# Block-sparse attention in a hybrid decoder step: the sliding branch's weights scaled by GpSimd instead of VectorE

## What is computed

```python
p_c = masked_softmax(q @ k_cmp, block_end <= t)         # compressed keys
p_s = masked_softmax(q @ k_sel, s <= t)                 # "full" here
p_w = masked_softmax(q @ k_win, (s <= t) & (s > t - WINDOW))   # WINDOW = 512
o = g_c * (p_c @ v_cmp) + g_s * (p_s @ v_sel) + g_w * (p_w @ v_win)
```

## Time and profile before

| what | value |
|---|---|
| time, median of 3 runs | 2090.6 us (2086.77 to 2098.51) |
| the profiled execution, its own time | 2094.56 us |
| its span in the trace | 2092.8 us |
| `attend_prompt` in that span | about 407 to 767 us |
| TensorE busy over the span | 1826.2 us, 87% |
| VectorE busy over the span | 1113.8 us, 53% |
| GpSimd busy over the span | 119.7 us, 6% |

### The profile page before, as it was taken

How to read it: one execution, slowest core, us unless ns; L and a number is a source line. 1 busy time by engine, 2 the same in 40 slices (tenths; PEclk the granted TensorE clock), 3 DMA queues, 4 the chain that set the end, 5 groups by cost and what they waited for, 6 DMA issues and landing times. The chain is left out here.

```text
span 2092.8 us, 32262 instructions
## 1 busy us (share of the span) xinstructions
PE 1826.2 (87%) x12951; PEld 1691.3 (81%) x12951; DVE 1113.8 (53%) x1980; ACT 634.8 (30%) x1134; POOL 119.7 (6%) x143
## 2 busy tenths in 40 slices
PE   6999999677888868988794458999999999999998
PEld 6989999566677757777682248999999999999997
DVE  5462752367777754555345665844444554444454
ACT  6523311244554442333223323521112111121211
POOL 0000000000000021221202120000000000000000
PEclk9999999768999988999856679999999999999999
DMA  7621243400000025446252646311211111111102
GB/s 186 87 91 31 88 145 112 101 11 21 11 12 1 1 103 179 172 162 215 94 127 40 184 138 205 86 36 44 77 40 40 40 40 40 64 56 40 40 21 81
DMA packets 171473, 170.87 MB, mean 82 GB/s; under 512 B 49756, under 2 KB 156340, under 8 KB 167396
## 3 DMA queue, kind: packets, MB, share of 16 engines
q1 hardware_dynamic: 167892, 131.54, 22.3%
q0 software_dynamic: 2304, 33.56, 4.2%
q10 hardware_dynamic: 1168, 4.26, 0.9%
HBM read 136.98 MB, written 36.56 MB: 83 GB/s over the span
## 5 line engine op out<-in xcount | busy, mean ns | idle before, releaser
L58 PE MATMUL pm<-hidH,weights 128*128 128x344 f32 x768 | 247.7, 323 | 4.4 <-DVE weights L3151 4.4
L58 PE MATMUL pm<-hH,wuH 128*128 128x344 f32 x768 | 246.4, 321 | 3.4 <-DVE wuL L3146 3.1
L59 PE MATMUL pm<-hidL,weights 128*128 128x344 f32 x768 | 246.7, 321 | 0.0
L60 PE MATMUL pm<-hidH,weights 128*128 128x344 f32 x768 | 246.3, 321 | 0.0
L60 PE MATMUL pm<-hH,wuL 128*128 128x344 f32 x768 | 245.4, 319 | 0.0
L59 PE MATMUL pm<-hL,wuH 128*128 128x344 f32 x768 | 245.2, 319 | 0.0
L58 PE MATMUL pz<-hH,winH 128*128 128x344 f32 x600 | 201.2, 335 | 11.0 <-DVE zb L830 6.5
L60 PE MATMUL pz<-hH,winL 128*128 128x344 f32 x600 | 194.9, 325 | 0.0
L59 PE MATMUL pz<-hL,winH 128*128 128x344 f32 x600 | 194.8, 325 | 0.0
L3155 DVE SCALAR_TENSOR_TENSOR act<-pm,onat 128x344 f32<-128x344 f32 x96 | 49.3, 515 | 244.6 <-PE pm L60 244.5
L3166 DVE TENSOR_TENSOR onat<-pm,onat 128x344 f32<-128x344 f32 x256 | 129.0, 513 | 70.3 <-PE pm L60 70.3
(11 more groups left out here) (588 smaller groups left out, 3582.3 us busy)
## 6 DMA issues: line engine op xcount, KB each, us to landing
uact<-in_w_up_dram SPq DMA_DIRECT2D x16, 1024.0 KB, 6.8
hs<-in_w_down_dram SPq DMA_DIRECT2D x16, 1024.0 KB, 4.9
raw<-in_w_in_dram SPq DMA_DIRECT2D x24, 512.0 KB, 4.0
vS_scratch<-page_rows SPq DMA_DIRECT2D x16, 512.0 KB, 4.5
hold<-vS_scratch SPq DMA_DIRECT2D x8, 1024.0 KB, 12.3
wo<-in_w_out_dram SPq DMA_DIRECT2D x12, 512.0 KB
act<-in_w_out_dram SPq DMA_DIRECT2D x12, 512.0 KB, 4.1
onat<-qkT_scratch SPq DMA_DIRECT2D x18, 256.0 KB, 4.1
```

What stands on the lines that cost most here:

```text
L58: nc.tensor.matmul(out, wH, mH, start=(k == 0), stop=False)
L59: nc.tensor.matmul(out, wH, mL, start=False, stop=False)
L60: last = nc.tensor.matmul(out, wL, mH, start=False, stop=(k == n - 1))
```

## The change

In the VectorE list, the reciprocals now carry a semaphore of their own (`rs_ready`), and only the FULL columns are scaled there; `scaled` is raised by that instruction. GpSimd gets a loop over all units and heads: it waits for the reciprocals of the head and scales the WIN columns, raising `win_scaled`. TensorE waits, as before, for `scaled` at a unit's first group, and in addition for `win_scaled` of both heads at each group whose last tile is a WIN tile. The order of TensorE's and ScalarE's instructions is the same.

```diff
@@ gpsimd, behind the masks
+                for u, (i, kv, j) in enumerate(sched.units):
+                    for g in range(2):
+                        pool.wait_ge(rs_ready, 2 * u + g + 1)
+                        at, w = TILES(i, FULL) * P, TILES(i, WIN) * P
+                        gate = (kv * 4 + 2 * j + g) * 3 + WIN
+                        nc.gpsimd.tensor_scalar(pm[:, u % 2, g, at:at + w], pm[:, u % 2, g, at:at + w], rs[:, u % 2, g, 1:2],
+                                                gnat[:, i, gate:gate + 1], ALU.mult, ALU.mult).then_inc(win_scaled, 1)
@@ tensor, turn(n)
                     if kind != CMP and n == first + 1:
                         pe.wait_ge(scaled, sched.scaled_at[u + 1])
+                    if kind != CMP and pair[-1][0] == WIN:
+                        pe.wait_ge(win_scaled, 2 * u + 2)
@@ vector, scale_head(s)
-                    nc.vector.reciprocal(rs[:, u % 2, g, :], den[:, u % 2, g, :])
+                    nc.vector.reciprocal(rs[:, u % 2, g, :], den[:, u % 2, g, :]).then_inc(rs_ready, 1)
                     nc.vector.drain()
-                    at = 0
-                    for b in (FULL, WIN):
-                        w = TILES(i, b) * P
-                        gate = (kv * 4 + 2 * j + g) * 3 + b
-                        last = nc.vector.tensor_scalar(pm[:, u % 2, g, at:at + w], pm[:, u % 2, g, at:at + w], rs[:, u % 2, g, b - 1:b],
-                                                       gnat[:, i, gate:gate + 1], ALU.mult, ALU.mult)
-                        at += w
-                    last.then_inc(scaled, 1)
+                    w = TILES(i, FULL) * P
+                    gate = (kv * 4 + 2 * j + g) * 3 + FULL
+                    nc.vector.tensor_scalar(pm[:, u % 2, g, 0:w], pm[:, u % 2, g, 0:w], rs[:, u % 2, g, 0:1],
+                                            gnat[:, i, gate:gate + 1], ALU.mult, ALU.mult).then_inc(scaled, 1)
```

More of the change, by code:

```diff
@@ L1170, in attend_prompt @@
         c_in, c_high, c_split, masks, masks_r = sem("c_in"), sem("c_high"), sem("c_split"), sem("masks"), sem("masks_r")
-        s_done, nm_ready, p_ready, scaled, pt_done, copied_a, copied_v, pv_done, o_used = (
-            sem("s_done"), sem("nm_ready"), sem("p_ready"), sem("scaled"), sem("pt_done"), sem("copied_a"), sem("copied_v"),
+        s_done, nm_ready, p_ready, scaled, rs_ready, win_scaled, pt_done, copied_a, copied_v, pv_done, o_used = (
+            sem("s_done"), sem("nm_ready"), sem("p_ready"), sem("scaled"), sem("rs_ready"), sem("win_scaled"), sem("pt_done"), sem("copied_a"), sem("copied_v"),
             sem("pv_done"), sem("o_used"))
```

## The result

The changed kernel takes 2069.3 us (median of 7 runs, 2066.11 to 2078.07), the kernel before 2086.8 us (median of its 7 runs, 2084.75 to 2098.51). The ratio is 0.9908, 95% interval 0.9884 to 0.9932: 19 us faster by the ratio, with 14 to 24 in the interval, and 17.5 us by the two medians. I had forecast 2081 us, 9.7 us faster, with 2073 as the lower end. Part of the distance to the range is the base: I had forecast from a median of 3 runs, 2090.6 us, and 7 runs give 2086.8; from that base the same lower end would have been 2069.

What follows compares the result with a forecast made beforehand. The attention stage was taken as a loop with VectorE's list most commonly late for TensorE; 10.7 us gained less 1 us took 9.7 us off 2094.6, giving 2084.9, or 2081 us at the median, range 2073 to 2107.

Steps and rivals of the forecast that it cites:

- VectorE's list shortened by 27.8 us: Attention stage: 64 WIN scalings leave VectorE, 33.6 us busy less 5.8 us overlap, or 0.43 us a head.
- VectorE first in the tie: After each head's reciprocals, VectorE's FULL scaling starts before GpSimd's and keeps its duration, about 0.68 us for 768 columns; 45%.
- GpSimd about 0.9 us for 640 columns: GpSimd's time for one WIN scaling, expected nearer its copy's rate, between bounds of 0.72 and 1.55 us.
- GpSimd's work hidden, about 1 us: Groups ahead of the WIN columns cover GpSimd's scaling; only tile 0 exposes it, counted as 1 us for tiles 0 to 3.
- Rival 3: WIN late: in tiles 0 to 3 WIN columns come 0.1 to 0.8 us later, eating the gain: 2091 us; 5%.
- Rival 1's price: GpSimd starts first and each FULL scaling ends behind GpSimd's: 2088 to 2112 us, halfway +8 us, 2099; 37%.
- the formula of the prediction: With GpSimd first, VectorE's list moves by GpSimd's total less 33.6 and 11.5 us: -8 to +32 us.
- What the gain can come from: Attention stage: only TensorE's idle time ending with something in VectorE's list, 55.7 us in 42 waits.
- the 8 and half of the other 34: TensorE's waits taken to shrink: 8 direct ones for a scaling and half the others, 25 × 0.43 = 10.7 us.
- The upper bound of the count: All 42 of TensorE's waits in the attention stage shrink by 0.43 us each: 18 us gained.

Runs made afterwards that it cites:

- e9: The changed kernel with a 2-column reciprocal into unused columns between VectorE's reciprocals and FULL scaling: 2092.2 us, ratio 1.0008 to the kernel before.
- e1: The changed kernel without GpSimd's loop and TensorE's wait for it, so nobody scales the WIN columns: 2065.4 us, ratio 0.9886 to the kernel before.
- e4: The changed kernel with a 2-column copy on VectorE ahead of the reciprocals: 2070.3 us, ratio 0.9903 to the kernel before.
- e11: The changed kernel with 60 identity products on TensorE ahead of its first wait in the mLSTM stage: 2082.4 us, ratio 0.9973 to the kernel before.
- e6: The kernel before with only query tiles 4 to 7 having their WIN columns scaled by GpSimd: 2073.9 us, ratio 0.9929.
- e5: The kernel before with only query tiles 0 to 3 having their WIN columns scaled by GpSimd: 2086.6 us, ratio 0.9963.
- e10: The kernel before with only the first head of each unit having its WIN scaling moved to GpSimd: 2074.8 us, ratio 0.9956.
- e7: The kernel before with only the second head of each unit having its WIN scaling moved to GpSimd: 2069.4 us, ratio 0.9918.
- e8: The changed kernel with the four CMP scalings of each CMP step moved to GpSimd as well: 2070.2 us, ratio 0.9879 to the kernel before.
- e3: The changed kernel with a 2-column copy on VectorE between the reciprocals and the FULL scaling: 2073.1 us, ratio 0.9936 to the kernel before.
- e12: e8 with 60 identity products on TensorE ahead of its first wait in the mLSTM stage: 2066.7 us, ratio 0.9902 to the kernel before.
- e2: The kernel before with each WIN scaling done a second time on VectorE into unused columns: 2109.9 us, ratio 1.0098.

## Why the prediction was half right

- *VectorE's list shortened by 27.8 us*: 27.6 in the trace of the stage. Right.
- *VectorE first in the tie, its FULL scalings unchanged*: right in 63 of 64 heads, 680 ns for 768 columns, mostly with 3 to 4 ns in hand. No row known beforehand decided this; I gave the forecast 45%, and the tie fell that way by luck. e9 shows that its other side is worth the whole gain.
- *GpSimd about 0.9 us for 640 columns*: 0.875 in e9, of which some may still be its own waiting.
- *GpSimd's work hidden, about 1 us*: 1.4 us in the stage by e1, within the difference of two traces. Rival 3 did not come.
- *Rival 1's price*: the sum said +8 us halfway between its ends; e9 gave +0.8 in the stage and 1.0008 in the ratio. The mechanism was as told, its size between the lower end and the middle. With e9's own durations by shape, 47.4 us of GpSimd for all heads, the formula of the prediction gives 47.4 - 33.6 - 11.5 = +2.3 us on VectorE.
- *What the gain can come from*: this step failed. "A gain there can come from TensorE's 55.7 us alone" put TensorE's busy time at nothing, without a reason. "I take the 8 and half of the other 34", 25 × 0.43 = 10.7 us, then sized the part in the waits, and the four kinds of waits did fall by 9.6 us (11.4, 11.0 and 11.3 in e1, e4 and e11). But the stage fell by 17.9, as TensorE's busy time fell by 10.9 us, at a granted clock of 0.92 instead of 0.88 (by 8 to 13 us in e1, e4 and e11). The upper bound of the count, 42 × 0.43 = 18, meets the 17.9 by coincidence: it is a sum over waits, and the waits gave half of it. I had also put the lower end of the range, 2073, where that bound lay, so no room was left for a term beside the waits.
- *Why the clock was higher* stays open. From the stage's first score product to the first of tile 4 the traces with VectorE's list unchanged there have a clock of 0.76 and 0.79 (before, e6), those with it shortened 0.81 to 0.84 (e1, e4, e5, e11, changed), and with one head of two moved 0.79 and 0.80 (e10, e7). That goes with the length of the list, but e9, where the gain is gone, has 0.82.
- *Most of the gain in which tiles*: not forecast; e5 and e6 give a share of 0.9 for the tiles where TensorE has much idle time and 0.5 to 0.6 where it is near full. A share by stretch of the earlier trace rows, for idle and busy time together, would have been the better term.

## What to carry over

When work leaves an engine whose list paces a loop, size the gain by a share of the removed time and not by the waits of another engine alone. Here it was about 0.9 where TensorE had idle time and 0.5 to 0.6 where it was near full, and 1.0 for the CMP scalings of e8. Leave room in the range for a different granted clock. Adding the same work once more tests in one run whether the list paces the stage; read its idle and busy time apart, as the lengths alone agreed here for different reasons. Before handing an elementwise SBUF operation to GpSimd beside a VectorE operation on SBUF that starts from the same event, find out which of the two starts first; a 0.17 us instruction between them decided over 18.7 us of the stage. If it can be chosen, the consumer's more urgent operation is to be the first.

## What I had not expected of the hardware

The contention goes by start order down to a few nanoseconds: VectorE 2 to 10 ns ahead won all of 63 heads, and 68 to 77 ns behind lost all 64 of e9. Back-to-back VectorE operations in SBUF can keep GpSimd out, or lose the place between them: with the 2-column copy of e3 it went 37 to 27, and what decides it is not shown.

The mLSTM stage, which no experiment but e11 and e12 touches, comes in two groups of lengths: 61.1, 60.8, 61.0, 61.7 and 64.5 us (the changed kernel, e6, e3, e10, e1) and 73.8, 73.7, 76.0, 75.7, 75.8, 76.0, 79.6 us (before, e2, e4, e5, e7, e9, e8). The windows over it, of the kernel before, of the changed kernel and of e8, show the same 274 products at different clocks:

```profile
1040.30:1114.10 73.80, 54.25 (x274) 46.75 (x274) 25.29 (x69) 15.14 (x41) 11.61 (x43) 0.59 0.49 122
```

```profile
1031.20:1092.20 61.00, 41.47 (x274) 35.17 (x274) 24.88 (x69) 15.08 (x41) 11.62 (x43) 0.75 0.59 147
```

```profile
1008.30:1087.90 79.60, 60.60 (x274) 52.64 (x274) 25.47 (x69) 15.39 (x42) 11.62 (x43) 0.52 0.46 114
```

At a mean of 0.59 or 0.52 TensorE spent most of the stage at 1.2 GHz, at 0.75 half of it at 2.4 GHz. This is 13 to 19 us, as much as the change itself. It would explain the two groups in the runs of e5 and e7, whose profiled executions (2089.3 and 2086.5 us, stage 75.7 and 75.8) are both of the upper group; no execution of their lower group was profiled, so this is not shown. Which kernel meets which length how often can't be read from one profile each; whether a little of the measured 19 us is of this kind, and whether e8 could be had at 2047 us in every run, stays open.
